# One-hot products on TensorE for the first expert block's rows, and routing and experts in one block

## The reference, cut to what matters

```python
scores = sigmoid(t @ router_w)                      # 16 experts in 4 groups
# the best group per token, the best two experts in it, weights w1, w2 that sum to 1
y = (silu(t @ wg[e]) * (t @ wu[e])) @ wd[e]         # D_EXPERT = 512
out = sum of w_k * y over the token's two experts
```

## Time and profile before

| | us |
|---|---|
| median of 3 runs (lowest, highest) | 1544.68 (1542.31, 1545.03) |
| the profiled execution, its own time | 1545.03 |
| its span, first to last instruction | 1543.3 |
| PE busy, share | 1303.0, 84% |
| DVE busy, share | 837.1, 54% |
| ACT busy, share | 667.9, 43% |
| POOL busy, share | 265.0, 17% |
| mean granted TensorE clock | 0.914 |

### The profile page before, as it was taken

One profiled execution on the slowest core, in us unless ns is written; L12 is line 12 of the kernel. 1 busy time (PEld: TensorE's weight loads), 2 busy tenths in 40 slices (PEclk: granted clock), 3 DMA queues, 4 the chain that ended last, 5 costly groups with the idle time before them and its releaser, 6 DMA issues. The chain is left out here.

```text
span 1543.3 us, 20591 instructions
## 1 busy us (share of the span) xinstructions
PE 1303.0 (84%) x7887; PEld 1154.0 (75%) x7887; DVE 837.1 (54%) x972; ACT 667.9 (43%) x1031; POOL 265.0 (17%) x285
## 2 busy tenths in 40 slices
PE   3999999979999999847889835998980899999970
PEld 1789999979999889845667724998860688888860
DVE  2411443276766111017687868233464599999956
ACT  2433321144343223137576738111140577777743
POOL 0600000000000101025599970000003000000002
PEclk9899999989999999968899965999985899999995
DMA  9991212021212433164455650321645599999935
GB/s 385 413 362 64 83 62 85 28 66 72 83 55 82 144 123 107 51 201 146 148 193 188 198 216 37 108 83 61 261 164 225 192 391 413 418 405 408 415 152 204
DMA packets 62497, 289.09 MB, mean 187 GB/s; under 512 B 9104, under 2 KB 13648, under 8 KB 42064
## 3 DMA queue, kind: packets, MB, share of 16 engines
q1 hardware_dynamic: 49424, 242.19, 42.1%
q0 software_dynamic: 12608, 45.62, 7.6%
q10 hardware_dynamic: 384, 0.16, 0.0%
HBM read 239.51 MB, written 48.43 MB: 187 GB/s over the span
## 5 line engine op out<-in xcount | busy, mean ns | idle before, releaser
L235 PE MATMUL banks<-rounded,rounded 128*128 128x320 f32 (+1 forms) x1152 | 359.6, 312 | 15.9 <-DVE rounded L214 9.6
L236 PE MATMUL banks<-rounded,rounded 128*128 128x320 f32 (+1 forms) x1152 | 357.7, 311 | 0.0
L237 PE MATMUL banks<-rounded,rounded 128*128 128x320 f32 (+1 forms) x1152 | 357.7, 311 | 0.0
L1999 DVE TENSOR_TENSOR rounded<-words,rounded 128x2048 fp32r<-128x2048 f32 x96 | 219.6, 2289 | 33.2 <-ACT rounded L1990 32.3
L214 DVE TENSOR_TENSOR rounded<-words,rounded 128x2048 fp32r<-128x2048 f32 x52 | 119.1, 2291 | 216.0 <-ACT rounded L206 216.0
L235 PEld LDWEIGHTS banks<-rounded,rounded 128*128 128x128 f32 (+1 forms) x1152 | 217.3, 189 | 16.9 <-issue 16.5
L236 PEld LDWEIGHTS banks<-rounded,rounded 128*128 128x128 f32 (+1 forms) x1152 | 217.2, 189 | 0.3
L237 PEld LDWEIGHTS banks<-rounded,rounded 128*128 128x128 f32 (+1 forms) x1152 | 217.0, 188 | 0.2
L1990 ACT ACTIVATE rounded<-words 128x2048 fp32r<-128x2048 f32 x96 | 183.9, 1916 | 47.5 <-PE banks L2115 39.7
L206 ACT ACTIVATE rounded<-words 128x2048 fp32r<-128x2048 f32 x52 | 99.2, 1908 | 125.4 <-PE banks L256 56.0
L1274 ACT ACTIVATE words<-words,words 128x128 f32<-128x128 f32 x320 | 97.7, 388 | 58.2 <-DMA words<-decay_sums 58.2
(11 more groups left out here) (275 smaller groups left out, 1996.0 us busy)
## 6 DMA issues: line engine op xcount, KB each, us to landing
words<-in_units SPq DMA_DIRECT2D x52, 1024.0 KB, 5.0
words<-in_wg SPq DMA_DIRECT2D x32, 1024.0 KB, 8.0
words<-in_wu SPq DMA_DIRECT2D x32, 1024.0 KB, 8.1
words<-in_wd SPq DMA_DIRECT2D x32, 1024.0 KB, 8.7
words<-decay_sums SPq DMA_DIRECT2D x40, 512.0 KB, 3.8
words<-in_w_mod_rest SPq DMA_DIRECT2D x32, 512.0 KB, 4.3
slot_rows<-words POOLq DMA_DIRECT2D x27, 512.0 KB, 21.7
expert_rows<-words POOLq DMA_DIRECT2D x25, 512.0 KB, 9.1
```

The costliest lines, as they stand in the source:

```text
L235: nc.tensor.matmul(out, lhs[0](k), rhs[0](k), start=(k == 0), stop=False)
L236: nc.tensor.matmul(out, lhs[0](k), rhs[1](k), start=False, stop=False)
L237: last = nc.tensor.matmul(out, lhs[1](k), rhs[0](k), start=False, stop=(k == nk - 1))
L1999: self.nc.vector.tensor_tensor(self.lo[:, q % 3, :], self.raw[q], self.hi[:, q % 3, :].bitcast(F32), ALU.subtract).then_inc(self.lo_ready, 1)
```

## The change

The one-hot matrices: `r.iota` holds 0 to 127 in each partition (a small transfer in `stage_out`). After the slot numbers are known, DVE compares `iota` with each token's two slot numbers (kept as floats in `chosen`), five `tensor_scalar` and five `scalar_tensor_tensor` of 128x128, which gives `first[:, c, :]`, a matrix with a one at (token, slot) where a token of chunk c has a slot below 128, that is, in block 0. PE multiplies each 128x128 piece of `h2` by it, eight pieces by five chunks, 40 float32 matmuls, and finds block 0's rows turned in banks 6 and 7, where the transposes put them before. `turn_rows(0, zero)` and the load of block 0's rows from `xs` are gone. The scatter itself stays, all ten transfers.

The block structure: routing and experts share one `nc.Block()`. Each engine's `inner` waits for `s_table`. SP no longer waits for the scatters in the routing part; it waits for them in the experts part, ahead of the load of block 1's rows and of unit 3 of block 1. The wait on `rows_turned` ahead of the load of block 2's rows is gone, since `XB[:, 0, :]` has no reader before it.

```diff
@@ stage_out, SP @@
             sp.dma_start(rw[:, :, 0:NE], io["router_w"].rearrange("p (k e) -> p k e", k=KD)).then_inc(s_rw, 16)
+            sp.dma_start(r.iota, io["iota"].partition_broadcast(P)).then_inc(s_iota, 16)
...
             sp.wait_ge(s_g2, 32)
+            sp.wait_ge(s_iota, 16)
@@ stage_route, SP @@
                 ex.load(sp, io, 1, q)
-            sp.wait_ge(s_sc, 16 * 2 * NC)
-            for u in range(2):
-                sp.dma_start(XB[:, u, :], xs[u]).then_inc(ex.rows_loaded[u], 16)
             sp.wait_ge(ex.lo_ready, 3)
             ex.load(sp, io, 1, 2)
@@ stage_route, DVE @@
-                do(nc.vector.tensor_reduce(five, tmp, AX.X, ALU.add))
+            do(nc.vector.tensor_reduce(chosen[:, k, :], tmp, AX.X, ALU.add))
                 if k == 0:
-                    do(nc.vector.tensor_copy(r.slot[k], five))
-            nc.vector.tensor_copy(r.slot[1], five).then_inc(s_ready, 1)
-            dve.wait_ge(s_ready, 1)
+                do(nc.vector.tensor_copy(r.slot[k], chosen[:, k, :]))
+        nc.vector.tensor_copy(r.slot[1], chosen[:, 1, :]).then_inc(s_ready, 1)
+        for c in range(NC):
+            nc.vector.tensor_scalar(first[:, c, :], r.iota, chosen[:, 0, c:c + 1], None, ALU.is_equal).then_inc(s_first, 1)
+        for c in range(NC):
+            dve.wait_ge(s_first, c + 1)
+            nc.vector.scalar_tensor_tensor(out=first[:, c, :], in0=r.iota, scalar=chosen[:, 1, c:c + 1], in1=first[:, c, :],
+                                           op0=ALU.is_equal, op1=ALU.add).then_inc(s_first, 1)
             ex.split_lo(dve, 0, zero, 2)
@@ stage_route, PE @@
             last.then_inc(s_pe, 1)
+        pe.wait_ge(s_first, 2 * NC)
+        for k in range(KD):
+            for c in range(NC):
+                last = nc.tensor.matmul(ps[:, 6 + k // 4, (k % 4) * P:(k % 4 + 1) * P], h2[:, c, k * P:(k + 1) * P], first[:, c, :],
+                                        start=(c == 0), stop=(c == NC - 1))
+        last.then_inc(ex.rows_turned, 1)
@@ stage_experts @@
+    def inner(eng):
+        eng.wait_ge(table_ready, 1)
+        return eng.value_load(r.table[0:1, NMB:NMB + 1], min_val=NE // 2 - 2, max_val=NMB // 2 - 2)
...
+        sp.wait_ge(*scattered)
+        sp.dma_start(XB[:, 1, :], xs[1]).then_inc(rows_loaded[1], 16)
             sp.wait_ge(ex.lo_ready, 4)
             ex.load(sp, io, 1, 3)
-            sp.wait_ge(rows_turned, 1)
             sp.dma_start(XB[:, 0, :], xs[2]).then_inc(rows_loaded[0], 16)
...
-                pe.wait_ge(rows_loaded[u], j.times(16, 16))
+            pe.wait_ge(rows_loaded[u], j.times(16, 16 * u))
...
-            turn_rows(0, zero)
             step(0, zero)
```

More of the change, by code:

```diff
@@ L1923, with _ @@
+    @block.gpsimd
+    def _(pool):
+        pool.wait_ge(s_ready, 1)
+        for c in range(NC):
+            for k in range(2):
+                pool.indirect_dma_start(out=scr["xs"], out_offset=bass.IndirectOffsetOnAxis(ap=r.slot[k][:, c:c + 1], axis=0),
+                                        in_=h2[:, c, :], in_offset=None).then_inc(s_sc, 16)
+    return block, s_table, (s_sc, 16 * 2 * NC)
 class Pair:
@@ L2014, in stage_experts @@
     rows_loaded, y_stored = ex.rows_loaded, [kit.sem(f"e_y_stored{u}") for u in range(2)]
[L2016 to L2017 removed]
+    rows_turned = ex.rows_turned
+    (rows_hi, rows_lo, silu, product, product_turned, product_hi, product_lo, y_low, y_high, y_free) = (
+        kit.sem("e_" + n) for n in ("rows_hi", "rows_lo", "silu", "product", "product_turned",
                                     "product_hi", "product_lo", "y_low", "y_high", "y_free"))
@@ new lines, in stage_experts, with _, load_step @@
+    block = Programs()
+    @block.sync
+    def _(sp):
+        n = inner(sp)
+        last_pair = Pair(n, 1)
+        sp.wait_ge(*scattered)
+        sp.dma_start(XB[:, 1, :], xs[1]).then_inc(rows_loaded[1], 16)
+        sp.wait_ge(ex.lo_ready, 4)
+        ex.load(sp, io, 1, 3)
+        sp.dma_start(XB[:, 0, :], xs[2]).then_inc(rows_loaded[0], 16)
+        def load_step(u, j, is_last=False):
+            e = expert(sp, j.times(2, u))
+            d = expert(sp, j.times(2, u - 1))
+            for q in range(6):
+                sp.wait_ge(ex.lo_ready, ex.index(u, j, q, -5))
+                ex.load(sp, io, e if q < 4 else d, q)
+                if q == 3 and not is_last:
+                    v, _ = after(u, j)
+                    sp.wait_ge(rows_turned, count(u, j, -1))
+                    sp.dma_start(XB[:, v, :], row(xs[bass.ds(j.times(2, u + 1), 1)])).then_inc(rows_loaded[v], 16)
+            return e
+        with sp.Fori(0, n) as i:
+            for u in range(2):
+                load_step(u, Pair(i, 1))
+        load_step(0, last_pair)
+        e = load_step(1, last_pair, is_last=True)
+        for q in (4, 5):
+            sp.wait_ge(ex.lo_ready, last_pair.times(12, 5 + q))
+            ex.load(sp, io, e, q)
+        last_rows = row(ys[bass.ds(last_pair.times(2, 1), 1)])
+        for h, ready in enumerate((y_low, y_high)):
+            sp.wait_ge(ready, count(1, last_pair))
+            sp.dma_start(last_rows[:, h * 512:(h + 1) * 512], YB[:, 1, h * 512:(h + 1) * 512]).then_inc(last_stored, 16)
+        sp.wait_ge(last_stored, 32)
@@ new lines, in _, with store @@
+    @block.gpsimd
+    def _(pool):
+        n = inner(pool)
+        def store(u, j):
+            pool.wait_ge(y_low, count(u, j))
+            pool.wait_ge(y_high, count(u, j))
+            pool.dma_start(row(ys[bass.ds(j.times(2, u), 1)]), YB[:, u, :]).then_inc(y_stored[u], 16)
+            pool.wait_ge(y_stored[u], j.times(16, 16))
+            pool.sem_inc(y_free, 1)
+        store(0, zero)
+        store(1, zero)
+        with pool.Fori(0, n) as i:
+            for u in range(2):
+                store(u, Pair(i, 1))
+        store(0, Pair(n, 1))
@@ L2279, in stage_combine @@
+    return block
 def stage_combine(kit, scr, out):
```

618 lines of the change are left out of this document (294 added, 324 removed).

## The result

| | before | changed |
|---|---|---|
| median, us (runs; lowest, highest) | 1544.6 (4; 1542.31, 1545.03) | 1532.37 (4; 1530.76, 1532.67) |
| ratio, 95% interval | | 0.9921 [0.9907, 0.9935] |
| the profiled execution, its span | 1545.03, 1543.3 | 1532.16, 1530.5 |
| mean granted TensorE clock | 0.914 | 0.923 |

The change makes the kernel 12.2 us faster. The forecast was 1532.8.

A forecast was written before the change was run, and what follows sets the result against it. PE bounds the steady part; before it PE idles 27.95 us until block 0's rows land. Earlier gate matmul 10.4 plus block 0's clock 1.5 make 11.9 off 1545.03, 1533.1; less 0.35 to the median, 1532.8; range 1528.5 to 1539.

The forecast's parts named there:

- One-hot matrices: Behind the slot numbers: ten DVE operations of 128x128 take 2.4 us, bounds 2.0 and 3.2, before PE is released.
- The products: Forty products, 80 records on PE, between one-hot matrices and block 0: 11.1 us, the clock rising from half within them.
- the case I had copied: L1145, same shape after a long idle time: 32 records in 6.00 us, taken as the products' first 32 records.
- Block 0's clock: Block 0's 48 matmuls: clock falls for 3.5 us, one in the gap before; 1.5 us gained, bounds 0 and 2.8.
- Added with no cost: The small transfer of 0 to 127, and the later table that every engine's `inner` waits for: no cost.
- Removed with no gain: The block boundary between routing and experts lay inside PE's idle time, so removing it gains nothing.
- What may be late next: Block 1's rows behind the scatters: landed at 1197.4, needed by 1202.4, so 5.0 us in hand despite 1 MB added.
- DVE beside POOL: Shared port held exclusively: 2.4 us more DVE work could put the scatters at most 2.4 later, the sum unchanged.
- the slow start of block 1: Block 1's start at half clock, 3.0 us, 1.5 lost; may be none or 5.7: -1.5 or +1.3 in the spread.
- The clock did not stay down: Rival, 6 in 100: clock stays at half through the products, 16.8 us instead of 11.1, only 4.7 off, 1540.0.
- the steady part is unchanged: Rival, 4 in 100: reordered loads leave PE waiting in 14 later steps; at 1.2 us each the kernel takes 1549.6.
- late rows: Rival, 6 in 100: block 1's rows come late, each us beyond the 5.0 costs one; 4.0 late gives 1536.8.

The follow-up runs named there:

- e9: The changed kernel with six unused float32 matmuls of 512 columns on PE between the rank products and the forty products: 1530.16 us, ratio 0.9907.
- e5: The changed kernel with all forty products issued twice over the same banks, same result: 1542.4 us, ratio 0.9996.
- e7: The changed kernel with 24 memsets, 11.5 us, on POOL ahead of its first scatter: 1537.27 us, ratio 0.9950.
- e2: The kernel before with only the small load of 0 to 127 added, which nothing uses: 1542.5 us, ratio 0.9988.
- e4: The changed kernel with routing and experts kept in two blocks, each ending in a barrier of all engines: 1546.09 us, ratio 1.0010.
- e13: e4 with twelve memsets, 5.7 us, on POOL behind the last scatter and ahead of the barrier: 1544.02 us, ratio 1.0008.
- e3: The changed kernel, one block, without one-hot matrices and products; block 0's rows scattered, loaded and transposed as before: 1546.64 us, ratio 1.0019.
- e10: The changed kernel with one-hot matrices and products made chunk by chunk, PE starting when chunk 0's matrix is there: 1533.87 us, ratio 0.9928.
- e8: The changed kernel with DVE's subtraction of weight unit 2 moved ahead of the slot numbers: 1533.52 us, ratio 0.9939.
- e1: The kernel before, unchanged, run and profiled again: 1544.74 us, ratio 1.0007.
- e6: The changed kernel with ten memsets, 4.8 us, on POOL ahead of its first scatter: 1532.23 us, ratio 0.9925.

## Why the prediction was right, step by step

The forecast and its mechanism held. The profile gives 9.3 us for the change where the sum said 11.9: the sum leaves out 2.7 that the changed kernel loses from block 1 on. That the medians differ by 12.2 is partly the variation ahead of the change. Beside the 1543 to 1544.3 that the longer series give for before, 1532.37 is 10.6 to 11.9 lower. So the mechanism was right, and that the forecast came within 0.5 us of the median is in part luck.

- **One-hot matrices.** 2.4 us, as taken (five of 1.06, five of 1.40, overlapped).
- **The products.** 10.76, with 11.1 forecast, but by two errors that nearly cancel. The pace at full clock is 0.115 a record in e9, not 0.103, so the 48 records taken at 5.1 us are worth 5.5. The clock rose 3.3 us after the first record, where it was 4.4 in the case I had copied, and half of the 1.1 comes back. That makes 10.95; the last 0.2 stays unexplained. Over seven profiles of the same forty products behind an idle PE they took 10.75 to 11.91, so the rise is not fixed to the start.
- **From the products to the gate matmul.** 2.42, unchanged. In sum 10.9 us for 10.4.
- **Block 0's clock.** It fell, and was back 3.6 us after the gate matmul began: 1.1 us gained for 1.5. The length of the fall was as assumed, its place was not: I had put 1 us of it in the gap, but it began 0.4 us after PE had resumed, so all of it was paid. In e5, e7 and e9 it stayed up behind the same 2.42 us; e5 and e9 show what that gives, 2.7, the other bound.
- **Added with no cost.** The small load: nothing (e2). The table and the wait of `inner`: nothing, since PE runs from the products to the gate matmul without a further wait.
- **Removed with no gain.** I said that the block boundary lay inside PE's idle time. In the kernel before that is so. But the step stopped short: with the products the boundary would have become the bound, 8.8 us behind POOL's last scatter (e4, e13). Merging alone, with its order of loads, costs 2.4 (e3), the products alone bring nothing (e4), and both together bring the gain. The sum came out right because it was made for both.
- **What may be late next.** The scatters to SP's load: before 18.25, e3 20.75, changed 22.5. So the added 1 MB cost 2.5 us (2.6 forecast) and DVE's work beside POOL about 1.7 (at most 2.4). e10 bears out the second: it has the same transfers and the same work on DVE, but POOL is held less (its tenth scatter is issued 12.45 us after the first, 14.23 in the changed kernel), and SP's load goes out 20.6 us after the first scatter. The rows landed 3.1 us after the issue at 1192.02, at 1195.1. ACT takes block 1's transposes at 1199.86, and they take 1.03, so they may start as late as 1198.8: 3.7 us in hand where I had 5.0. e7 overdrew this and paid.
- **DVE beside POOL.** A scatter that begins inside a DVE operation on two tensors, or in a run of them without a gap, ends 0.8 to 0.9 us after it: before 1176.07 with the subtraction over at 1175.13, changed 1174.59 (1173.73), e8 1176.99 (one-hot operations over at 1176.13). In e7 the ninth scatter, far from routing, does it again:

```profile
1195.34 2.85 POOL L1938 DMA_INDIRECT slot_rows<-words,words  x1 [0.30 <-issue]
...
1195.07 2.29 DVE L2020 TENSOR_TENSOR rounded<-words,rounded 128x2048 fp32r<-128x2048 f32 x1 [5.12 <-ACT rounded L2011]
```

  It ends at 1198.19, the subtraction at 1197.36. In e10, where DVE waits between the small operations, the scatter beside them takes 0.99. Nor does every operation do it: the first scatter of the changed kernel begins at 1169.53, among the five TENSOR_SCALAR, and takes 1.06. So operations on two tensors stop POOL while they run without a gap, and the loss is theirs, not the transfers'. This agrees with the Trainium skill (Trainium Architecture — The Big Picture, What this means for kernel authors), that DVE and GpSimd lock their shared port and do not divide it. It cost nothing because of the 3.7 us in hand.
- **Not in the sum.** From block 1 on the changed kernel loses 2.45 us. 1.2 of it is the slow start of block 1: 5.4 us at half clock (1203.5 to 1208.9) where it was 3.0; the range had it. About 1.1 is a wait before the last `down`. ACT waits 4.47 us for a w_down unit, before it was 3.21; PE then stands 7.17 us instead of 6.03. The unit was in use 6.23 us after its issue, before 4.98:

```profile
1466.31 3.05 SPq L1985 DMA_DIRECT2D words<-in_wd  x2
...
1472.54 1.91 ACT L2007 ACTIVATE rounded<-words 128x2048 fp32r<-128x2048 f32 x1 [4.47 <-DMA words<-in_wd]
```

  Whether this belongs to the change stays open: the idle time is 5.9 to 6.4 in before, e1, e2, e3 and e5, 6.5 to 7.3 in the other kernels without added matmuls there, e4 among them, which starts block 0 as late as before. No run took it apart.
- **The rivals.** The clock did not stay down, the steady part is unchanged, and late rows cost time only where e7 forced them; in e9 PE waited 0.75 us for them without a loss.

## What to carry to other kernels

When a wait on a transfer is taken off a path, look for the next barrier behind which the same transfer is awaited: here the end of a block held all engines until POOL's scatters had landed, so that the product on TensorE was worth nothing until the block was merged, and the merge alone, with its order of loads, was a loss. When work moves to an engine that has been idle, count the gaps around it at both clock levels: nineteen matmuls into unused banks in four gaps, with the products made chunk by chunk, gave as much here (10 us) as the whole change. To judge a change of less than 1%, measure in the trace from the last point that the change doesn't touch, since what lies ahead of it varied by 9 us.

## What the runs showed of the hardware

- At the end of a block POOL's DRAIN was over 0.5 us after its last indirect transfer had landed (before, e4, e13), and the other engines were held until then: in e4 ACT started 8.8 us after that transfer had been issued. 5.66 us of other work on POOL in that time cost nothing (e13).
- Behind the same 2.42 us of idle PE the clock fell in the changed kernel, e6, e8 and e10, and stayed up in e5, e7 and e9. In e7 it had come out of half clock only some 9 us before the gate matmul, as in e6, so what PE did before doesn't tell them apart. Where the clock fell, it did so 0.4 to 1.4 us after PE had resumed. I found no row that tells which it will be.
- A float32 product of 128x128, two records, takes 0.23 us at full clock in a run of forty (9.20 us), more than the 0.206 of five such products in the earlier trace rows.
- An indirect scatter of 512 KB takes POOL 0.96 us, and up to 3.69 us beside DVE operations on two tensors that follow each other without a gap; beside TENSOR_SCALAR operations it took 1.06.
